# ScalarE's order inside a step of stick-breaking attention: exp and ln ahead of the upper part, the copy of the scores two steps ahead and behind it

## The chip, the cores and the metric

The kernel runs on one core of one Trainium2 chip. The metric is the device time of one execution in microseconds (us); lower is better. The engines are named as the profile names them: PE is TensorE (matmuls; PEld its weight loads), ACT is ScalarE, DVE is VectorE, POOL is GpSimd, SP is SyncE, which issues nearly all DMAs.

## The reference, cut to what matters

One decoder layer over 1024 positions and 1024 channels: RMSNorm, one wide input projection, three mixers (gated gMLP, gated DeltaNet, stick-breaking attention), a gated sum of their outputs, an output projection and a feed-forward part. The change touches only the attention:

```python
z = einsum('bthd,bshd->bhts', q, k) * dh ** -0.5            # 8 heads of 64
log_keep = where(causal, log_sigmoid(-z), 0)                # = -softplus(z)
later = cumsum(log_keep, axis=3, reverse=True) - log_keep
w = where(causal, exp(log_sigmoid(z) + later), 0)
o = einsum('bhts,bshd->bthd', w, v)
```

Here t is the query position, s the key position, and the sum runs over the keys between them.

## The kernel before, in words

Every matrix product in the kernel is done with three fp32r matmuls: each operand is split into an upper and a lower part, and high*high, high*low and low*high are added up. One core does everything, in phases. The second phase is the attention. It is a loop of four turns, each over two heads (u = 0, 1). A turn walks 12 blocks, `BLOCKS`: for queries 0 to 511 (T = 0) the key blocks j = 3, 2, 1, 0 of 128 keys, then for queries 512 to 1023 (T = 1) the key blocks 7 down to 0. A block has one step for each head, so a turn has 24 steps, `STEPS`. Step 2x and step 2x+1 belong to block x. A step's tiles are [128 keys, up to 512 queries]; on the diagonal only the queries that can see the keys are taken, so the widths by block are 128, 256, 384, 512, and again 128, 256, 384, 512, 512, 512, 512, 512.

The work of one step y goes around the engines like this (names as in the code, lines as in the profile):

- PE `scores` (L989 mask, L992): both steps of a block at once, into one of three PSUM banks `s_bank[y % 3]` each.
- ACT `copy_z` (L709): scores times 0.125 into `a_z[y % 4]`. It waits for the scores (`z_ready`), and from step 4 on for `argument(y - 4)`, which is the last reader of that buffer (`arg_ready`).
- DVE `minus_abs` (L1250): -|z| into `a_e[y % 3]`.
- ACT `exp_z` (L714) and `ln_z` (L719): ln(1 + exp(-|z|)), in place.
- DVE `softplus` (L1257): max(z, 0) plus that, into `a_sp`.
- ACT `upper_sp` (L726) and DVE `lower_sp` (L1263): the two fp32r parts of it.
- PE `sums_from` (L1002, L1003): the running sum over keys with a triangular matrix, and later `sums_rest` (L1010, L1011) for what the triangle left out.
- DVE `argument` (L1272): z minus the running sum, into `a_A`.
- ACT `exp_arg` (L732): its exp, the weights.
- PE `weighted_values` (L1021): once per block, two blocks later.

The orders in which the engines take these are written out by hand, and each engine keeps to its own. In loop turn y (28 of them, `NST + LAG`):

- DVE does `lower_sp(y-1)`, `argument(y-2)`, `minus_abs(y+1)`, `softplus(y)`.
- PE does `sums_rest(y-3)`, `sums_from(y-1)`, two or three steps (6 to 9 matmuls of 512 columns) of the input projection that runs beside the attention (`pe_beside`, L306 to L308), and in every even y also `weighted_values(y/2-2)` and then `scores(y/2+1)`.
- ACT does the order that the change edits, and now and then its share of the projection beside (`act_beside`): it takes half a block of results out of PSUM (`stage`, L332; behind y = 3, 6, 10, 13, 17, 20, 24, 27), and behind y = 6, 13, 20 and 27 also splits the next weights (`w_hi`, L294), which DVE's `w_lo` (L298) waits for.

Of the kernel before, what the change touches and what calls it, by code (L numbers as in the profile page):

```python
# [54 lines left out]
def hybrid_decoder_layer(nc, xT, w_stream, w_bd, w_spT, cols_in, consts_in, outT):  # L55
# [17 lines left out]
    with top:  # L73
# [343 lines left out]
        def act_beside(act, b):  # L417
            for step in b.steps():
                blk, r = divmod(step, 16)
                n, s = b.n0 + blk // 2, blk % 2  # L420
                if r == 7:
                    take_projection(act, n, s, 0, b.funcs[blk // 2])
                if r == 15:
                    take_projection(act, n, s, 1, b.funcs[blk // 2])
                    if b.funcs[blk // 2] == ACT.Gelu and s == 1:
                        exp_ln_tables()
                    split_hi(act, n + 1, s)
# [65 lines left out]
        NST = len(STEPS)  # L493
# [4 lines left out]
        def cols_of(y):  # L498
            return slice(first_col(STEPS[y][0], STEPS[y][2]), HALF)
# [159 lines left out]
        def _(act):  # L659
# [36 lines left out]
            with act.Fori(0, 4) as i:  # L696
                b = Beside(PAIR_AT + 2 * i, AT_SLOTS, (ACT.Identity,) * 2)
                act_beside(act, b)

                for hf in range(2):  # L700
                    act.wait_ge(at_vt, 2 * i + hf + 1)
                    nc.scalar.activation(a_v[:, 4 * hf:4 * hf + 4, :], z_bank[hf][:].rearrange("p (n c) -> p n c", c=P),
                                         ACT.Copy).then_inc(at_v, 1)

                def copy_z(y):
                    act.wait_ge(z_ready, 1 + NST * i + y + 1)
                    if y >= 4:
                        act.wait_ge(arg_ready, NST * i + y - 3)
                    nc.scalar.activation(a_z[y % 4][:, cols_of(y)], s_bank[y % 3][:, cols_of(y)], ACT.Copy, scale=0.125).then_inc(z_read, 1)  # L709

                def exp_z(y):
                    e = a_e[y % 3][:, cols_of(y)]
                    act.wait_ge(na_ready, NST * i + y + 1)
                    nc.scalar.activation(e, e, ACT.Exp).then_inc(e_ready, 1)  # L714

                def ln_z(y):
                    e = a_e[y % 3][:, cols_of(y)]
                    act.wait_ge(e_ready, NST * i + y + 1)
                    nc.scalar.activation(e, e, ACT.Ln, bias=1.0).then_inc(l_ready, 1)  # L719

                def upper_sp(y):
                    act.wait_ge(sp_ready, NST * i + y + 1)
                    if y >= 4:
                        act.wait_ge(cum_ready, NST * i + y - 3)
                        act.wait_ge(rest_done, N_REST * i + RESTS[y - 3])
                    nc.scalar.activation(a_sp_hi[y % 4][:, cols_of(y)], a_sp[y % 3][:, cols_of(y)], ACT.Copy).then_inc(sp_hi_ready, 1)  # L726

                def exp_arg(y):
                    T, u, j = STEPS[y]
                    act.wait_ge(arg_ready, NST * i + y + 1)  # L730
                    a = a_A[u][(y // 2) % 2][:, cols_of(y)]
                    nc.scalar.activation(a, a, ACT.Exp).then_inc(a_ready, 1)  # L732

                def out_av(T):
                    act.wait_ge(av_done, 2 + NBK * i + 4 * (2 * T + 1))
                    act.wait_ge(y_stored[T], 1 + 16 * i)
                    nc.scalar.activation(a_y[T][:], o_bank[:], ACT.Copy).then_inc(av_read, 1)
                    act.wait_ge(av_read, 1 + 2 * i + T + 1)
                    act.dma_start(yT[8 + i, :, HALF * T:HALF * T + HALF], a_y[T][:]).then_inc(y_stored[T], 16)

                copy_z(0)
                for y in range(NST + LAG):
                    if 1 <= y < NST + 1:
                        upper_sp(y - 1)
                    if y < NST:
                        exp_z(y)
                    if y + 1 < NST:
                        copy_z(y + 1)
                    if y < NST:
                        ln_z(y)  # L750
                    if 2 <= y < NST + 2:
                        exp_arg(y - 2)
                    act_beside(act, b)
                    if y == 11:
                        out_av(0)
                out_av(1)
# [875 lines left out]
```

## Time and profile before

| | |
|---|---|
| median of 3 runs | 2322.13 us (2322.05 to 2327.91) |
| profiled execution | 2324.92 us |
| its span, first to last instruction | 2323.1 us |
| mean granted TensorE clock | 0.955 of full speed |
| PE busy / DVE busy / ACT busy | 2112.4 / 906.6 / 814.1 us |
| attention, from the first copy of scores to the last `stage` | about 203.4 to 621 us, four turns of about 107 us |

Busy times are of the whole span; a matmul counts as busy until its modelled end, so a busy PE isn't one at its peak. The attention is 18% of the span; all else in the kernel is the same in both versions.

### The profile page before, as it was taken

Reading aid. Unit: us, or ns where it says so; the run is one execution under the profiler, and the core shown is the slowest. Engines: PE = TensorE matmul, PEld = TensorE weight load, DVE = VectorE, ACT = ScalarE, POOL = GpSimd, SP = SyncE. Lnnn points to the kernel's source line nnn. Section 1 sums busy time; section 2 is a strip of 40 time slices with the busy share of each in tenths; the row PEclk is TensorE's granted clock in tenths of the full one; section 3 lists DMA queues with packets and bytes.
Section 4 is the critical chain, followed back from the end, with each engine's and each line's share of the span. In section 5 each row is a group of like instructions: output and inputs, shape, how many; then the busy total and the mean of one; then the engine's idle time right before and its main releaser. Section 6 shows DMA issues by size and latency. Waiting matters only on the chain.

```text
span 2323.1 us, 26938 instructions
## 1 busy us (share of the span) xinstructions
PE 2112.4 (91%) x9786; PEld 1639.2 (71%) x9786; DVE 906.6 (39%) x1229; ACT 814.1 (35%) x1297; POOL 126.6 (5%) x79
## 2 busy tenths in 40 slices
PE   6998888888999999999979899977999999999994
PEld 3885555555678787877747688845888888888883
DVE  4113535354462534436223556245322322322335
ACT  4224646565633534334223433233301302302311
POOL 2000000000012030302100000022000000000002
PEclk7998999898999999999989999987999999999997
DMA  3222111212121212112042443311111111111113
GB/s 119 101 81 82 42 68 41 72 44 72 67 103 37 99 36 92 61 54 72 18 190 90 182 136 120 134 74 44 45 54 45 45 54 45 45 54 45 45 45 145
DMA packets 51530, 174.16 MB, mean 75 GB/s; under 512 B 5536, under 2 KB 5536, under 8 KB 51488
## 3 DMA queue, kind: packets, MB, share of 16 engines
q1 hardware_dynamic: 50336, 171.52, 20.7%
q10 hardware_dynamic: 1152, 2.10, 0.2%
q8 instruction: 25, 0.41, 0.1%
q14 instruction: 17, 0.14, 0.0%
HBM read 127.45 MB, written 46.14 MB: 75 GB/s over the span
## 4 chain that ended last, share of the span: by engine, by line
PE 67%; DVE 8%; ACT 5%; DMA 4%; issue 4%; SPq 1%; POOL 1%; ACTq 0%; DVEq 0%; POOLq 0%
PE gemm L306 16%; PE gemm L308 16%; PE gemm L307 16%; DMA w_raw<-w_stream 2%; PE dn L1091 2%; PE dn L1089 2%; PE gemm L1170 2%; PE gemm L1171 1%; PE gemm L1172 1%; PE attn_out L1021 1%; ACT w_hi L294 1%; DVE d_cv L1306 1%; PE z L992 1%; DMA a_k<-projections 1%; DVE a_sp_lo L1263 1%
## 5 line engine op out<-in xcount | busy, mean ns | idle before, releaser
L306 PE MATMUL gemm<-act_hi,w_hi 128*128 128x512 f32 x1600 | 667.1, 417 | 40.4 <-DVE act_lo L469 16.2
L308 PE MATMUL gemm<-act_hi,w_lo 128*128 128x512 f32 x1600 | 636.5, 398 | 0.0
L307 PE MATMUL gemm<-act_lo,w_hi 128*128 128x512 f32 x1600 | 636.2, 398 | 0.0
L306 PEld LDWEIGHTS gemm<-act_hi,w_hi 128*128 128x128 f32 x1600 | 307.5, 192 | 125.1 <-issue 36.7
L308 PEld LDWEIGHTS gemm<-act_hi,w_lo 128*128 128x128 f32 x1600 | 307.5, 192 | 67.5
L298 DVE TENSOR_TENSOR w_lo<-w_raw,w_hi 128x1024 fp32r<-128x1024 f32 x144 | 177.5, 1233 | 452.5 <-ACT w_hi L294 447.7
L307 PEld LDWEIGHTS gemm<-act_lo,w_hi 128*128 128x128 f32 x1600 | 308.8, 193 | 61.6 <-issue 6.5
L294 ACT ACTIVATE w_hi<-w_raw 128x1024 fp32r<-128x1024 f32 x144 | 151.4, 1052 | 334.6 <-PE gemm L308 281.5
L332 ACT ACTIVATE stage<-gemm,cols 128x512 f32<-128x512 f32 x120 | 82.2, 686 | 338.1 <-PE gemm L308 332.6
L306 PE MATMUL gemm<-f_hi,w_hi 128*128 128x512 f32 x512 | 199.2, 389 | 0.0
L307 PE MATMUL gemm<-f_lo,w_hi 128*128 128x512 f32 x512 | 199.2, 389 | 0.0
L308 PE MATMUL gemm<-f_hi,w_lo 128*128 128x512 f32 x512 | 199.2, 389 | 0.0
L1541 POOL TENSOR_TENSOR d_bB<-d_at,consts 128x512 f32<-128x512 f32 x48 | 64.4, 1356 | 993.3 <-DVE d_at L1352 905.8
L306 PEld LDWEIGHTS gemm<-f_hi,w_hi 128*128 128x128 f32 x512 | 96.1, 188 | 20.0
L307 PEld LDWEIGHTS gemm<-f_lo,w_hi 128*128 128x128 f32 x512 | 96.1, 188 | 20.0
L308 PEld LDWEIGHTS gemm<-f_hi,w_lo 128*128 128x128 f32 x512 | 96.1, 188 | 19.9
L1479 DVE TENSOR_TENSOR f_t<-f_t 128x512 f32<-128x512 f32 x64 | 44.3, 692 | 162.7 <-ACT f_t L908 162.7
L908 ACT ACTIVATE f_t<-gemm 128x512 f32<-128x512 f32 x64 | 38.3, 599 | 189.0 <-PE gemm L308 189.0
L1493 DVE TENSOR_TENSOR mixed<-mixed,gemm 128x512 f32 (+1 forms) x48 | 33.0, 688 | 175.3 <-PE gemm L308 175.2
L1250 DVE SCALAR_TENSOR_TENSOR a_e<-a_z 128x512 f32<-128x512 f32 (+3 forms) x96 | 53.4, 556 | 89.2 <-ACT a_z L709 88.2
L1170 PE MATMUL gemm<-y_hi,w_hi 128*128 128x512 f32 x192 | 77.3, 403 | 9.7 <-DVE y_lo L370 7.6
L1263 DVE TENSOR_TENSOR a_sp_lo<-a_sp,a_sp_hi 128x512 fp32r<-128x512 f32 (+3 forms) x96 | 53.5, 558 | 66.3 <-ACT a_sp_hi L726 66.3
(225 smaller groups left out, 2506.3 us busy)
## 6 DMA issues: line engine op xcount, KB each, us to landing
w_raw<-w_stream SPq DMA_DIRECT2D x144, 512.0 KB, 3.5
projections<-stage SPq DMA_DIRECT2D x60, 512.0 KB, 2.9
gate<-projections SPq DMA_DIRECT2D x48, 256.0 KB, 2.8
d_in<-projections SPq DMA_DIRECT2D x12, 512.0 KB, 4.5
y_lo<-branch_outputs SPq DMA_DIRECT2D x6, 1024.0 KB, 12.0
x_sb<-xT SPq DMA_DIRECT2D x4, 1024.0 KB, 8.6
x_fin<-xT SPq DMA_DIRECT2D x4, 1024.0 KB, 8.0
residual<-mixed SPq DMA_DIRECT2D x8, 512.0 KB, 2.6
```

The lines of the kernel that those rows point to most:

```text
L294: nc.scalar.activation(w_hi[s][:], w_raw[s][:].rearrange("p (k c) -> p k c", k=KT), ACT.Copy).then_inc(hi_ready[s], 1)
L298: nc.vector.tensor_tensor(w_lo[s][:], w_raw[s][:].rearrange("p (k c) -> p k c", k=KT), w_hi[s][:].bitcast(f32), ALU.subtract).then_inc(lo_ ...
L306: nc.tensor.matmul(g_bank[hf][:], w_hi[s][:, k, :], a_hi[:, k, t], start=(k == 0), stop=False)
L307: nc.tensor.matmul(g_bank[hf][:], w_hi[s][:, k, :], a_lo[:, k, t], start=False, stop=False)
L308: last = nc.tensor.matmul(g_bank[hf][:], w_lo[s][:, k, :], a_hi[:, k, t], start=False, stop=(k == KT - 1))
L332: nc.scalar.activation(stage[s][:, HALF * hf:HALF * hf + HALF], g_bank[hf][:], func, bias=cols[:, ds(V_BIN + 2 * n + s, 1)]).then_inc(bank ...
L1089: last = nc.tensor.matmul(o, d_B[:, n, :], d_T[:, n, :], start=True, stop=True)
L1091: last = nc.tensor.matmul(o, d_X[:, n, :], d_TT[:, n, :], start=True, stop=True)
L1170: nc.tensor.matmul(g_bank[hf][:], w_hi[s][:, kk, :], y_upper(y)[:, t], start=(k == 0), stop=False)
L1250: nc.vector.scalar_tensor_tensor(a_e[y % 3][:, t], z[:, t], -1.0, z[:, t], ALU.mult, ALU.min).then_inc(na_ready, 1)
L1263: nc.vector.tensor_tensor(a_sp_lo[y % 4][:, t], a_sp[y % 3][:, t], a_sp_hi[y % 4][:, t].bitcast(f32), ALU.subtract).then_inc(sp_lo_ready, 1)
L1541: nc.gpsimd.tensor_tensor(d_B[:, c, :], d_at[:, c, :], consts[:, None, C_LEV + lev, :].broadcast_to([P, 4, P]), ALU.mult).then_inc(dn_b[g], 1)
```

## The change

The order of ACT in loop turn y of the attention is another one. Before: `upper_sp(y-1)`, `exp_z(y)`, `copy_z(y+1)`, `ln_z(y)`, `exp_arg(y-2)`. After: `exp_z(y)`, `ln_z(y)`, `upper_sp(y-1)`, `copy_z(y+2)`, `exp_arg(y-2)`. The copy of step 1 moves ahead of the loop, beside that of step 0. No instruction is added or removed, and neither the waits that an operation carries nor the orders of PE, DVE, POOL and SP are edited.

```diff
                 copy_z(0)
+                copy_z(1)
                 for y in range(NST + LAG):
+                    if y < NST:
+                        exp_z(y)
+                        ln_z(y)
                     if 1 <= y < NST + 1:
                         upper_sp(y - 1)
-                    if y < NST:
-                        exp_z(y)
-                    if y + 1 < NST:
-                        copy_z(y + 1)
-                    if y < NST:
-                        ln_z(y)
+                    if y + 2 < NST:
+                        copy_z(y + 2)
                     if 2 <= y < NST + 2:
                         exp_arg(y - 2)
                     act_beside(act, b)
```

## Rows read from the trace of the kernel before

**Rows 1.** The page: busy time of the engines over the span.
```profile
PE 2112.4 (91%) x9786; PEld 1639.2 (71%) x9786; DVE 906.6 (39%) x1229; ACT 814.1 (35%) x1297; POOL 126.6 (5%) x79
```

**Rows 2.** Waits of PE, whole span: us in total, times, longest.
```profile
PE dn L1002 <- DVE a_sp_lo L1263: 25.3, 24, 3.3
...
PE cumsum L1002 <- DVE a_sp_lo L1263: 11.4, 8, 1.9
```

**Rows 3.** Timeline of all engines, second turn: start, duration in us, idle before it.
```profile
366.59 0.60 ACT L709 ACTIVATE a_z<-z 128x512 f32<-128x512 f32 x1 [0.80 <-PE dn L992]
...
368.63 0.63 ACT L726 ACTIVATE a_sp_hi<-a_sp 128x512 fp32r<-128x512 f32 x1 [0.51 <-DVE a_sp L1257]
...
369.29 0.69 DVE L1263 TENSOR_TENSOR a_sp_lo<-a_sp,a_sp_hi 128x512 fp32r<-128x512 f32 x1 [0.78 <-ACT a_sp_hi L726]
...
369.90 0.68 DVE L1272 TENSOR_TENSOR a_A<-a_z,cumsum 128x512 f32<-128x512 f32 x1
...
370.04 0.51 PE L1002 MATMUL dn<-a_sp_hi,a_from 128*128 128x512 f32 x1
...
371.10 0.68 DVE L1257 SCALAR_TENSOR_TENSOR a_sp<-a_z,a_e 128x512 f32<-128x512 f32 x1
...
371.90 0.63 ACT L726 ACTIVATE a_sp_hi<-a_sp 128x512 fp32r<-128x512 f32 x1 [0.59 <-DVE a_sp L1257]
...
374.03 0.60 ACT L709 ACTIVATE a_z<-z 128x512 f32<-128x512 f32 x1 [0.99 <-PE z L992]
...
374.53 0.62 ACT L719 ACTIVATE a_e<-a_e 128x512 f32<-128x512 f32 x1
...
375.27 0.68 DVE L1257 SCALAR_TENSOR_TENSOR a_sp<-a_z,a_e 128x512 f32<-128x512 f32 x1
```

**Rows 4.** Groups of ACT in 314 to 403 us: busy, mean ns, idle before.
```profile
L726 ACT ACTIVATE a_sp_hi<-a_sp 128x512 fp32r<-128x512 f32 x12 | 7.5, 628 | 4.5 <-DVE a_sp L1257 4.4
...
L714 ACT ACTIVATE a_e<-a_e 128x512 f32<-128x512 f32 x12 | 7.4, 616 | 0.0
L732 ACT ACTIVATE a_A<-a_A 128x512 f32<-128x512 f32 x11 | 6.9, 626 | 2.8 <-DVE a_A L1272 2.8
L332 ACT ACTIVATE stage<-gemm,cols 128x512 f32<-128x512 f32 x7 | 4.8, 688 | 5.7 <-PE gemm L308 5.7
...
L294 ACT ACTIVATE w_hi<-w_raw 128x1024 fp32r<-128x1024 f32 x3 | 3.1, 1046 | 0.0
...
L714 ACT ACTIVATE a_e<-a_e 128x128 f32<-128x128 f32 x4 | 1.2, 298 | 0.4 <-DVE a_e L1250 0.4
```

**Rows 5.** Timeline of ACT alone, second turn, its first and last block.
```profile
318.02 0.38 ACT L709 ACTIVATE a_z<-dn 128x256 f32<-128x256 f32 x1 [1.37 <-PE z L992]
...
319.10 0.31 ACT L726 ACTIVATE a_sp_hi<-a_sp 128x128 fp32r<-128x128 f32 x1 [0.49 <-DVE a_sp L1257]
...
393.43 0.63 ACT L726 ACTIVATE a_sp_hi<-a_sp 128x512 fp32r<-128x512 f32 x1 [0.65 <-DVE a_sp L1257]
```

**Rows 6.** Stretches: length, busy (x count) of PE, PEld, DVE, ACT, POOL, granted clock, DMA share, GB/s.
```profile
229.00:232.00 3.00, 3.00 (x9) 2.31 (x8) 1.82 (x5) 2.19 (x7) 0.00 (x0) 0.55 0.02 8
256.00:259.00 3.00, 3.00 (x10) 0.80 (x8) 1.16 (x2) 1.06 (x2) 0.00 (x0) 0.50 0.02 10
359.00:362.00 3.00, 0.60 (x4) 0.35 (x2) 0.85 (x2) 2.50 (x5) 0.00 (x0) 1.00 0.21 85
403.00:411.00 8.00, 8.00 (x34) 4.74 (x32) 0.00 (x0) 1.39 (x3) 0.00 (x0) 1.00 0.00 0
```

**Rows 7.** The chain that ended last, first turn, block 7 to 8.
```profile
254.19 0.44 PE dn L1002
...
259.45 0.59 ACT a_z L709
```

**Rows 8.** The same chain, second turn, the same place.
```profile
362.91 0.44 PE dn L1002
...
366.61 0.59 ACT a_z L709
```

## The prediction, made before the changed kernel was run

> **What bounds the kernel now.** I read the page first. PE is busy 91% of the span and ACT 35% [rows 1]. So ACT's order can matter only where PE waits for ACT. The waits view says where. In the attention PE waits for the running sum's operand, the lower part, 25.3 + 11.4 = 36.7 us in 32 waits [rows 2]. The reader should see in it that PE already follows a ring of ACT and DVE in this stage.
>
> The timeline gives the ring [rows 3]. Take a loop turn with even y = 16, all tiles 512 wide. `upper_sp(15)` starts at 368.63, `lower_sp(15)` at 369.29, `sums_from(15)` at 370.04. Behind it on PE stand the projection's matmuls, `weighted_values` and the scores of the next block. The copy of those scores, `copy_z(18)`, starts at 374.03, having waited for exactly them. Call the time from `upper_sp(y-1)` to `copy_z(y+2)` A; here A = 5.40 us. Then DVE, which keeps its order, does `minus_abs(18)` and `softplus(17)`, the latter from 375.27 to 375.95, and 0.12 later the next odd `upper_sp` could start (371.10 + 0.68 to 371.90 is that 0.12). So the way back, B, is 376.07 - 374.03 = 2.04 us, and the ring is A + B = 7.44. The copies of this block and the one before it start at 366.59 and 374.03, also 7.44 apart. The ring explains the time in full.
>
> **The change part by part.** Nothing is added or removed, so no duration enters on its own: the price is what stands behind what. The rule of the new order is that in an even turn `copy_z(y+2)` stands directly behind `upper_sp(y-1)`. Its scores come from PE's end of the same turn y, which needs that very `upper_sp(y-1)`. PE's order isn't edited, so A stays, and ACT now idles through nearly all of it. Before, ACT did `exp_z(y)`, `copy_z(y+1)`, `ln_z(y)`, `exp_arg(y-2)`, `upper_sp(y)` and `exp_z(y+1)` in that time and waited only 0.99 [rows 3]. All this now starts behind the copy, and `upper_sp(y)` with it, which DVE and PE wait for.
>
> The new way back B, at full width, from the start of `copy_z(y+2)`. Queued ACT instructions start 0.50 (behind a copy, 374.03 to 374.53) to 0.52 apart, 0.10 less than their 616 to 628 ns [rows 3, 4]. An instruction that needs the result before it starts 0.03 after its end (`upper_sp` to `lower_sp`: 0.66).
> - copy 0.50, `exp_arg(y-2)` 0.52, `exp_z(y+1)` 0.65 (ln needs it), `ln_z(y+1)` 0.52: `upper_sp(y)` starts at 2.19.
> - `lower_sp(y)` starts 0.66 later, at 2.85. DVE's `argument(y-1)` stands behind it, 0.61 later, at 3.46, and ends at 4.14 (0.68).
> - `copy_z(y+3)` overwrites the tile that `argument(y-1)` reads, so it waits for that: 0.11 later, 4.25. (Before, the copy ran one step ahead only, and this wait was long met.)
> - copy 0.50, `exp_arg(y-1)` 0.52, `exp_z(y+2)` 0.65, `ln_z(y+2)` 0.52: `upper_sp(y+1)` starts at 6.43. `minus_abs(y+2)` ended at 4.74, before its exp; `softplus(y+1)` is done too.
>
> So B goes from 2.04 to 6.43, and the ring from 7.44 to 11.83: 4.39 us more for each full block.
>
> Narrower blocks: an ACT instruction takes 298 ns at 128 columns against 616 at 512 [rows 4], the four widths lying on a line. In the above, by width 128/256/384/512, the terms of the copied block are 0.96/1.36/1.80/2.17, those of the block being argued 0.81/1.14/1.50/1.83, those of the block between 1.09/1.52/1.98/2.43. For blocks x = 1 to 10 this makes B = 4.13, 5.29, 4.89, 4.28, 4.13, 5.29, 6.10, 6.43, 6.43, 6.43, together 53.4. A, read off at the same ten places of the second turn as from 368.63 to 374.03 [rows 3], is 3.6, 4.5, 4.4, 5.3, 4.7, 4.5, 5.6, 5.4, 5.6, 5.6, together 49.1.
>
> ACT's share of the projection now lies wholly on the ring: six `stage` at 0.59 and three `w_hi` at 0.95 inside it (688 and 1046 ns less 0.10 [rows 4]), 6.4 us. In the odd turns y = 3, 13, 17 `stage` also waits about 0.4 for PE's late projection, 1.2. The output copy behind y = 11 costs 1.2, as it did. With 0.3 for the clock still low at the start, the ten rings take 53.4 + 49.1 + 6.4 + 1.2 + 1.2 + 0.3 = 111.6 us from `upper_sp(1)` to `upper_sp(21)`. Before it is 393.43 - 319.10 = 74.3 [rows 5]. That is 37.3 us more.
>
> Start: `copy_z(2)` stays at 318.02 (its scores aren't moved) [rows 5]. Now `exp_z(1)`, `ln_z(1)`, `upper_sp(0)`, `lower_sp(0)`, `minus_abs(2)`, `exp_z(2)`, `ln_z(2)` stand between it and `upper_sp(1)`, some 2.7 us at these widths, so that starts at 320.75 instead of 319.10: 1.65 more. `copy_z(1)` ahead of the loop costs nothing: ACT idled there.
>
> End: nothing. From `upper_sp(21)` on no copies are left, and PE has its two turns of matmuls and four of projection to do without a gap (8.00 busy of 8.00 in the last stretch [rows 6]); ACT's last `exp_arg` comes at 10.8 after `upper_sp(21)` by the steps above, PE asks for it at 13.9. DMAs: ACT's output store moves with its copy, weight loads and stores on SP are a turn ahead; all have more time, not less. The next heads' loads start at the end of the turn, as before, so the 10 us between turns stay.
>
> One turn: 37.3 + 1.65 = 39.0; four turns 156 us.
>
> **The clock.** PE's idle stretches grow. After the scores PE now waits for `lower_sp(y)`: 2.85 + 0.75 behind the copy less 0.46 of `sums_rest`, 3.1 us at full width, at least 2 in each narrower ring, and up to 4.6 where `w_hi` falls in, all against a longest wait of 3.3 before [rows 2]. The trace before shows both outcomes of such a wait. Behind those at 226 and 250 us the granted clock was 0.55 and 0.50, so the lower level of 1.2 GHz; behind the 3.3 us at 359 it stayed at 1.00 [rows 6]. I count four falls behind the eight waits of 1.9 us and more in the four turns (in each, one of 1.9 and one of 3.3 [rows 2]). The price is to be had from one place in two turns: from `sums_from` to the copy 259.45 - 254.19 = 5.26 with a fall, 366.61 - 362.91 = 3.70 without [rows 7, 8], so 1.6 us. Now there are ten such waits in a turn, 40 in all. With half of them followed by a fall, and half of the falls spent behind `sums_from(y)`, where PE has some 1.7 us to spare before `upper_sp(y+1)`, that is 10 x 1.6 = 16, less the four falls already in the time, 6: 10 us. Bounds: -6 (no fall any more) and 40 x 1.6 = 64.
>
> The Trainium skill ("TensorE: Matmul & The Clock Gate", on the oscillation of the gate in real kernels) goes further: it says that idle gaps between bursts of matmuls bring PE back to the half rate again and again, every burst starting cold. This case's rows agree only in part, since one of the two 3.3 us waits left the clock at 1.00. By the page the sum would be at the upper bound or the second rival below, not at 10.
>
> **Sum.** 2324.9 (profiled) + 156 + 10 = 2491 us. The median of the runs lies 2.8 lower, so I say 2490.
>
> **The rivals.**
> - *The clock never comes back.* The whole of A runs at 1.2 GHz in every ring. At full width A has 3.96 us of PE in it, some 2.5 of them matmul streaming that doubles; over the ten rings and four turns about 100 us. For it: half the waits before were followed by a fall. Against: after each fall the next three us were back at 1.00, and at the low clock PE idles less. Time 2325 + 156 + 100 = 2580.
> - *The second copy doesn't hold.* If `copy_z(y+3)` and what follows it is not held up by `argument(y-1)` (its wait is met in time because DVE is ahead of my steps), B is 1.5 shorter at full width, about 1.2 on average: 40 x 1.2 = 48 less, 2440. Against: `argument(y-1)` is queued behind `lower_sp(y)` on DVE, and that needs `upper_sp(y)`.
> - *Faster: the DVE detour vanishes.* Before, `softplus` stood behind `minus_abs` and so behind the late copy (B). With ln two steps from the copy, `upper_sp` no longer needs the new scores. If the scores were there when the copy's turn comes, PE would lose all its waits for the lower part, 36.7 us [rows 2]: 2288. It decides at one point: the scores must come within about 0.5 us after `upper_sp(y-1)`, and the 5.40 measured has PE's whole turn in it, which depends on this `upper_sp`. I see no way to that.
> - *Nothing changes*: the waits only swap places. The ring would have to be set by PE; but PE waited in it 32 times.
>
> **Chances and range.** The forecast as summed, 2460 to 2540: 0.62. Clock low throughout or nearly so, above 2540: 0.17. Second copy not held, or other steps shorter, 2400 to 2460: 0.15. Slower, but by less than that: 0.02. Faster 0.02, no change 0.02. A measurement of this kernel can tell 0.3%, 7 us, from no change. So slower 0.96, same 0.02, faster 0.02. The range for 8 in 10 takes the neighbours partly in: 2430 to 2560.
>
> **What the changed profile would show.** In even turns ACT idles 4 to 5 us for the scores (L992), directly behind `upper_sp` (L726), not about 1; the full-width copies of consecutive blocks start 11.8 apart without projection work; PE's waits at L1002 for `a_sp_lo` go from 36.7 us to somewhere between 110 and 190, with 3 us at a full block; each turn of the loop takes 39 us more and the span before 203 us and after the attention stays as it was. The second copy waits for `a_A` of DVE (L1272). The clock falls inside the four turns some 20 times, not four. If ACT does not wait right behind `upper_sp` in the even turns, the mechanism is wrong; if it does and the pitch isn't near 11.8, a term of B is.

## The result, and the profile after

| | before | changed |
|---|---|---|
| median of the runs | 2322.09 us (2321.42 to 2327.91, 4 runs) | 2515.58 us (2512.83 to 2519.29, 4 runs) |
| span of the profiled execution | 2323.1 us | 2511.0 us |
| mean granted TensorE clock | 0.955 | 0.925 |

The changed kernel is slower: ratio 1.0828, 95% interval 1.0806 to 1.0851, so 193 us more. The forecast was 2490 (range 2430 to 2560), 166 us more.

First the page of the changed kernel: the busy times of DVE, ACT and POOL are those of before [rows 1] within 1%. PE's reads 76 us more and its weight loads' 49 us more.

```profile
PE 2188.1 (87%) x9786; PEld 1688.1 (67%) x9786; DVE 902.9 (36%) x1229; ACT 820.8 (33%) x1297; POOL 126.6 (5%) x79
```

The instructions are as many as before, so single matmuls took longer, and that goes with the lower granted clock. The stretches (columns as in [rows 6]) show where: ahead of the attention and behind it PE is as busy as it was, for as long. First the changed kernel, then the one before.

```profile
0.00:199.00 199.00, 172.10 (x682) 131.86 (x683) 41.51 (x36) 59.94 (x77) 12.95 (x10) 0.91 0.28 101
811.00:2511.00 1700.00, 1576.25 (x7542) 1273.64 (x7541) 653.77 (x794) 500.88 (x681) 113.65 (x69) 0.97 0.22 77
199.00:811.00 612.00, 439.73 (x1567) 282.56 (x1566) 207.66 (x399) 259.96 (x540) 0.00 (x0) 0.81 0.11 38
```

```profile
0.00:200.00 200.00, 172.79 (x684) 131.74 (x685) 41.50 (x36) 60.18 (x78) 12.95 (x10) 0.91 0.28 102
621.00:2323.00 1702.00, 1578.54 (x7545) 1276.06 (x7543) 653.55 (x795) 501.17 (x681) 113.70 (x69) 0.97 0.22 77
200.00:621.00 421.00, 361.08 (x1561) 231.44 (x1560) 211.56 (x399) 252.77 (x539) 0.00 (x0) 0.94 0.15 55
```

The attention went from 421 to 612 us, and its granted clock from 0.94 to 0.81. Those 191 us are the whole loss. The waits of the changed kernel answer to [rows 2]: us in total, times, longest.

```profile
ACT a_z L709 <- PE z L992: 140.3, 32, 6.8
...
PE cumsum L1002 <- DVE a_sp_lo L1263: 122.3, 44, 4.5
...
ACT a_z L709 <- PE dn L992: 89.1, 16, 7.2
...
ACT a_z L709 <- DVE a_A L1272: 45.5, 40, 1.4
...
PE dn L1002 <- DVE a_sp_lo L1263: 28.0, 17, 3.8
```

PE's waits for the lower part went from 36.7 to 150.3 us, and ACT stands 229 us in front of copies waiting for scores (61 before). The third kind of wait on `a_z` is new: 40 times, once a ring, a copy waits for `argument`.

The timeline of one full-width ring in the changed kernel answers to [rows 3].

```profile
459.87 0.61 ACT L726 ACTIVATE a_sp_hi<-a_sp 128x512 fp32r<-128x512 f32 x1
...
466.94 0.60 ACT L709 ACTIVATE a_z<-dn 128x512 f32<-128x512 f32 x1 [6.46 <-PE z L992]
...
467.44 0.62 ACT L732 ACTIVATE a_A<-a_A 128x512 f32<-128x512 f32 x1
467.95 0.62 ACT L714 ACTIVATE a_e<-a_e 128x512 f32<-128x512 f32 x1
468.61 0.63 ACT L719 ACTIVATE a_e<-a_e 128x512 f32<-128x512 f32 x1
469.14 0.61 ACT L726 ACTIVATE a_sp_hi<-a_sp 128x512 fp32r<-128x512 f32 x1
469.79 0.69 DVE L1263 TENSOR_TENSOR a_sp_lo<-a_sp,a_sp_hi 128x512 fp32r<-128x512 f32 x1 [6.78 <-ACT a_sp_hi L726]
470.39 0.68 DVE L1272 TENSOR_TENSOR a_A<-a_z,dn 128x512 f32<-128x512 f32 x1
470.53 0.50 PE L1002 MATMUL cumsum<-a_sp_hi,a_from 128*128 128x512 f32 x1 [2.96 <-DVE a_sp_lo L1263]
...
471.17 0.60 ACT L709 ACTIVATE a_z<-z 128x512 f32<-128x512 f32 x1 [1.42 <-DVE a_A L1272]
...
473.37 0.61 ACT L726 ACTIVATE a_sp_hi<-a_sp 128x512 fp32r<-128x512 f32 x1
```

Read it downwards from the copy at 466.94. It comes directly behind an upper part (459.87) and a wait of 6.46 us. From there the second upper part starts at 2.20, its lower part at 2.85, `argument` at 3.45, the second copy at 4.23 behind a wait of 1.42, and the next upper part at 6.43. The prediction had 2.19, 2.85, 3.46, 4.25 and 6.43. So B is as worked out. But A is 7.07 us here, not 5.4 to 5.6: that is the clock, as the experiment e4 shows below.

### The profile page after: what moved, and what is told of

Its sections match the earlier page's. It is cut to its first block, busy times and chain, and to the rows that moved or that the text cites. A ratio compares the mean times of both kernels' runs of the same rounds, so it can differ in the third digit from the quotient of the medians.

```text
span 2511.0 us, 26938 instructions
## 1 busy us (share of the span) xinstructions
PE 2188.1 (87%) x9786; PEld 1688.1 (67%) x9786; DVE 902.9 (36%) x1229; ACT 820.8 (33%) x1297; POOL 126.6 (5%) x79
## 4 chain that ended last, share of the span: by engine, by line
PE 66%; ACT 8%; DVE 7%; issue 4%; DMA 4%; SPq 1%; POOL 1%; ACTq 0%; DVEq 0%; POOLq 0%
PE gemm L306 16%; PE gemm L307 15%; PE gemm L308 15%; DMA w_raw<-w_stream 2%; PE dn L1091 2%; PE attn_out L1021 2%; PE dn L1089 1%; PE gemm L1170 1%; PE gemm L1172 1%; PE gemm L1171 1%; PE z L992 1%; ACT a_sp_hi L726 1%; DVE a_sp_lo L1263 1%; ACT w_hi L294 1%; ACT a_e L714 1%
## 5 line engine op out<-in xcount | busy, mean ns | idle before, releaser
L306 PE MATMUL gemm<-act_hi,w_hi 128*128 128x512 f32 x1600 | 687.0, 429 | 40.3 <-DVE act_lo L469 16.2
L308 PE MATMUL gemm<-act_hi,w_lo 128*128 128x512 f32 x1600 | 655.4, 410 | 0.0
L307 PE MATMUL gemm<-act_lo,w_hi 128*128 128x512 f32 x1600 | 655.3, 410 | 0.0
L306 PEld LDWEIGHTS gemm<-act_hi,w_hi 128*128 128x128 f32 x1600 | 319.7, 200 | 128.6 <-issue 37.0
L308 PEld LDWEIGHTS gemm<-act_hi,w_lo 128*128 128x128 f32 x1600 | 319.3, 200 | 72.0
L307 PEld LDWEIGHTS gemm<-act_lo,w_hi 128*128 128x128 f32 x1600 | 320.8, 200 | 64.8 <-issue 6.5
L1002 PE MATMUL cumsum<-a_sp_hi,a_from 128*128 128x512 f32 (+3 forms) x48 | 25.7, 536 | 122.3 <-DVE a_sp_lo L1263 122.3
L1002 PEld LDWEIGHTS cumsum<-a_sp_hi,a_from 128*128 128x128 f32 x48 | 10.5, 220 | 138.2 <-DVE a_sp_lo L1263 138.2
```

What stands on the lines that cost most here:

```text
L306: nc.tensor.matmul(g_bank[hf][:], w_hi[s][:, k, :], a_hi[:, k, t], start=(k == 0), stop=False)
L307: nc.tensor.matmul(g_bank[hf][:], w_hi[s][:, k, :], a_lo[:, k, t], start=False, stop=False)
L308: last = nc.tensor.matmul(g_bank[hf][:], w_lo[s][:, k, :], a_hi[:, k, t], start=False, stop=(k == KT - 1))
```

## The experiments

For each kernel A and B were read from the timeline at the ten rings (x = 1 to 10) of all four turns and summed. A is the time from an odd step's upper part to the late copy, B the way back to the next odd step's upper part. "Low clock" is the time at the lower level, added up from stretches of 1 us over the attention; "falls" are separate low stretches inside the turns, not counting the one that every turn begins with.

| kernel | median us | ratio to before | A, 40 rings | B, 40 rings | low clock, us | falls |
|---|---|---|---|---|---|---|
| before | 2322 | 1 | 211.5 | 92.1 | 52 | 4 |
| changed | 2515.6 | 1.0828 | 230.8 | 256.9 | 235 | 44 |
| e1, order alone | 2360.6 | 1.0164 | 222.9 | 118.5 | 75 | 9 |
| e2, depth alone | 2482.5 | 1.0688 | 228.4 | 228.4 | 202 | 34 |
| e3, late copy half a ring on | 2366.2 | 1.0193 | 219.8 | 124.2 | 71 | 9 |
| e4, PE kept busy | 2488.7 | 1.0725 | 209.9 | 249.4 | 84 | 11 |
| e5, five a_z tiles | 2498.8 | 1.0764 | 224.9 | 249.1 | 204 | 39 |
| e10, exp_arg first | 2479.6 | 1.0701 | 219.7 | 234.2 | 163 | 23 |

**Order or depth.** The change does two things: it puts exp and ln ahead of the upper part, and it copies two steps ahead. e1 and e2 do one each.

```diff
 # e1: order alone
+                    exp_z(y); ln_z(y)
                     upper_sp(y - 1)
-                    exp_z(y); copy_z(y + 1); ln_z(y)
+                    copy_z(y + 1)
 # e2: depth alone
+                copy_z(1)
...
-                        copy_z(y + 1)
+                        copy_z(y + 2)
```

> The order alone: exp, ln, upper part, then the copy only ONE step on (y+1), exp_arg. Theory (the copy of the scores in an even turn stands directly behind the upper part that those scores depend on, so ACT's work can't overlap PE's): here the late copy stands in the odd turn again, with exp, ln and the next upper part ahead of it, so A stays overlapped. Only minus_abs, exp and ln now lie between copy and next upper part: B = 0.63 + 0.79 + 0.65 + 0.52 = 2.6 instead of 2.04, 0.55 x 40 rings = 22 us, about 2345. Rival (exp and ln ahead of the upper part are what costs): near the changed kernel, 2480 to 2515.

> The depth alone: the old order (upper part, exp, copy, ln, exp_arg), but the copy is that of step y+2. Theory: in even turns the late copy again stands behind the upper part that its scores depend on, and ln(y), exp_arg, upper(y) wait behind it. By the steps of the prediction B = 5.98 at full width against 6.43 in the changed kernel, 0.45 x 40 = 18 us less than the changed kernel's 2516: about 2498. Rival (the order is what costs): near 2322 to 2345.

e1 took 2360.6 us (ratio 1.0164, interval 1.0146 to 1.0182), e2 2482.5 (1.0688, 1.0667 to 1.0709). The depth is what costs: alone it makes 162 of the 193 us, the order alone 40 (both against 2320.9 us, the kernel before measured beside them). Both numbers missed by some 15, e1 above and e2 below what was expected. In e1 B at full width is 2.56 (2.6 expected), but in the rings of the odd turns y = 3, 13 and 17, which have a `stage` in them, it grew by 1.0 to 1.2: B is 26 more in all (22 expected), A 11 more. In e2 B at full width is 5.94 (5.98 expected); what it is below the expectation comes mostly from the ring of y = 13, 6.5 to 8.1 where the changed kernel has 9.1 to 9.3, and that of y = 17. Two long waits on ACT stand in the timeline of a full-width ring of e2:

```profile
441.06 0.60 ACT L709 ACTIVATE a_z<-z 128x512 f32<-128x512 f32 x1 [4.26 <-PE z L993]
...
445.06 0.60 ACT L709 ACTIVATE a_z<-z 128x512 f32<-128x512 f32 x1 [0.90 <-DVE a_A L1273]
```

The wait for the scores is 4.26, against 4.98 in a ring of the changed kernel at full clock, since exp(y) now runs in it. Where the late copy stands decides more than the order of the rest.

**Half a ring.** e3 keeps the changed kernel's order and its total depth, and takes only the copy that waits for new scores out of the even turn.

```diff
-                    if y + 2 < NST:
-                        copy_z(y + 2)
+                    if y % 2 and y + 1 < NST:
+                        copy_z(y + 1)
+                        copy_z(y + 2)
```

> The changed kernel with one instruction moved by half a ring: the even turn's copy(y+2) is taken at the same place of the following odd turn, ahead of that turn's own copy(y+2); the even turn has none. Theory: exp_arg, exp, ln and the next upper part run during A again; B = 2.7 (two copies, exp_arg, exp, ln), 0.65 x 40 = 26 us over before: about 2348. Rival (the second copy's wait for argument, or exp and ln first, is the main cost): 2450 or more.

e3 took 2366.2 us (1.0193, 1.0176 to 1.021). One instruction moved by a turn of the loop gives back 149 of 193 us. In its timeline the second copy comes with no wait of its own, since the second upper part, its lower part and `argument` were done during A:

```profile
382.83 0.61 ACT L726 ACTIVATE a_sp_hi<-a_sp 128x512 fp32r<-128x512 f32 x1
385.63 0.60 ACT L709 ACTIVATE a_z<-z 128x512 f32<-128x512 f32 x1 [2.19 <-PE dn L993]
386.13 0.59 ACT L709 ACTIVATE a_z<-dn 128x512 f32<-128x512 f32 x1
```

This is the place of the loss, shown by taking it away. The time is 18 us above what was expected, which stays open in part: of the 45 us over the kernel before, B makes 32 (26 expected) and A 8 (none expected).

**The clock.** e4 adds matmuls whose results nobody reads, ahead of `sums_from`.

```diff
+                    if 3 <= y < NST - 1:
+                        keep_awake(y if y % 2 else y - 1, 9 if y % 2 else 5)
                     if 1 <= y < NST + 1:
                         sums_from(y - 1)
...
+                def keep_awake(y, count):
+                    pe.wait_ge(z_read, NST * i + y + 1)
+                    for _ in range(count):
+                        nc.tensor.matmul(s_bank[y % 3][:], a_from[:], act_hi[:, 0, 0:HALF], start=True, stop=True, ...)
```

> The changed kernel plus matmuls that nobody reads (9 in each odd turn, 5 in each even turn, 512 columns, ahead of sums_from), placed where PE idles, into the score bank whose copies are done. Theory: some 35 us of the 193 is the granted clock, which falls in the idle stretches and makes A longer (A sums to 54 to 60 us in a turn against 49 forecast); with PE busy the falls go and the time is 2475 to 2485. Rival 1 (the falls are spent where PE has time to spare): 2510 to 2520. Rival 2 (the added matmuls delay sums_from more than the clock gives back): above 2520.

e4 took 2488.7 us (1.0725, 1.0707 to 1.0743). More work made it 27 us faster, which ends 4 us above the expected range. The falls went from 44 to 11, A from 230.8 to 209.9, B from 256.9 to 249.4. The timeline is of the same ring as the one shown above: from upper part to late copy 5.59 us instead of 7.07, and the wait for the scores 4.98 instead of 6.46. The 9 added matmuls stand in what was an idle stretch of 2.96.

```profile
450.17 0.61 ACT L726 ACTIVATE a_sp_hi<-a_sp 128x512 fp32r<-128x512 f32 x1
...
455.76 0.60 ACT L709 ACTIVATE a_z<-dn 128x512 f32<-128x512 f32 x1 [4.98 <-PE z L992]
...
456.23 2.22 PE L1030 MATMUL z<-act_hi,a_from 128*128 128x512 f32 x9
...
459.36 0.50 PE L1002 MATMUL cumsum<-a_sp_hi,a_from 128*128 128x512 f32 x1 [0.91 <-DVE a_sp_lo L1272]
```

**The terms of B.** e5 takes the second copy's wait away, with a fifth `a_z` tile (all `y % 4` of it become `y % 5`); e10 moves `exp_arg(y-2)` ahead of the copy.

```diff
 # e5
-                    if y >= 4:
-                        act.wait_ge(arg_ready, NST * i + y - 3)
+                    if y >= 5:
+                        act.wait_ge(arg_ready, NST * i + y - 4)
 # e10
+                    if 2 <= y < NST + 2:
+                        exp_arg(y - 2)
                     if y + 2 < NST:
                         copy_z(y + 2)
-                    if 2 <= y < NST + 2:
-                        exp_arg(y - 2)
```

> The changed kernel with five a_z tiles instead of four, so that copy(y+3) no longer waits for argument(y-1). By the steps of B that wait costs little: copy(y+3) starts at 2.71 instead of 4.25, but exp_arg(y-1) behind it waits for the same argument, until 4.25, where it stood at 4.75. B 5.94 instead of 6.43, 0.49 x 40 = 20 us less than the changed kernel: about 2496. Rival (the prediction's second rival as it was priced, 1.2 to 1.5 a ring): 2456 to 2468.

> The changed kernel with exp_arg(y-2) ahead of copy(y+2). A check of the bookkeeping of B: in the even turn exp_arg runs while ACT would wait for the scores anyway, one slot of 0.52 less behind the copy at full width (0.2 to 0.5 by width). In the odd turn nothing changes, since both wait for argument(y-1). B 5.9 instead of 6.43, some 0.4 x 40 = 16 us less than the changed kernel: about 2500. Rival (B isn't a plain sum of what stands behind the copy): no change, 2516.

e5 took 2498.8 us (1.0764, 1.0748 to 1.078), 17 less than the changed kernel. The timeline shows why so little: the copy is early, and `exp_arg` behind it takes up the wait.

```profile
311.85 0.58 ACT L709 ACTIVATE a_z<-z 128x512 f32<-128x512 f32 x1
313.30 0.63 ACT L732 ACTIVATE a_A<-a_A 128x512 f32<-128x512 f32 x1 [0.87 <-DVE a_A L1272]
```

B there is 5.97 at full width (5.94 expected).

e10 took 2479.6 us (1.0701, 1.0659 to 1.0744), 36 less where 16 were expected. B at full width is 5.85, as worked out. Over 40 rings B gives 23, of it 7 in the rings of y = 13 (7.5 instead of 9.1 to 9.3), and A gives 11. There are 21 falls fewer. Why moving `exp_arg` spares falls was not tested.

**A faster kernel.** Four versions start from the kernel before. All swap `softplus` and `minus_abs` on DVE, so that the next upper part doesn't wait for the late copy by way of DVE.

```diff
 # DVE, all four
+                    if y < NST:
+                        softplus(y)
                     if y + 1 < NST:
                         minus_abs(y + 1)
-                    if y < NST:
-                        softplus(y)
 # ACT in e6: upper_sp(y-1), exp_z(y), ln_z(y), exp_arg(y-2), copy_z(y+1)
 # e7: copy_z(y+1) ahead of exp_arg(y-2)
 # e8: as e6, and act_beside of turn y-1 behind exp_z(y)
 # e9: as e8, and ahead of the wait for vT_loaded 22 matmuls that nobody reads
```

> A try at a faster kernel, from the ring of the one before: DVE takes softplus(y) ahead of minus_abs(y+1), and ACT takes upper(y-1), exp(y), ln(y), exp_arg(y-2), copy(y+1). The way from the late copy through minus_abs and softplus to the next upper part (B = 2.04) shrinks to one ACT slot, 0.5; then PE sets the pitch, some 6.75 by its own starts against 7.44. 0.7 x 40 = 28 us less at most, the waits behind stage and w_hi stay: about 2297. Rival (PE or the clock already sets the pitch): 2315 to 2325.

> As e6, but with the copy ahead of exp_arg, so B is 1.02 instead of 0.5. If the ring through ACT still sets the pitch this is some 0.3 to 0.5 a ring slower than e6, 2310; if PE does, the two are equal within 5 us.

> As e6, but ACT's share of the projection (stage, w_hi) of turn y is done in turn y+1 behind the upper part and exp, where PE no longer waits for it. The two long waits of a turn, 1.9 and 3.3 us, go, 5.2 x 4 = 21 us, and with them the four falls of the clock, 6: about 2272. Rival (these waits hide behind PE's own work or come back as a wait of DVE's w_lo): as e6.

> The kernel of e8 with 22 matmuls that nobody reads in the wait for the next heads' values between two turns (some 5 us of 5.5). The clock should then be at its upper level for the transposes, the first scores and the first projection steps, which ran at the lower one: some 6 to 7 us of PE work at half rate in e8's trace, 2 to 3 us less a turn, 8 to 10 in all: about 2300. Rival (a DMA or ACT sets this stretch): as e8, 2309.

| kernel | median us | ratio to before | interval |
|---|---|---|---|
| e6 | 2313.4 | 0.9962 | 0.9948 to 0.9976 |
| e7 | 2314.5 | 0.9964 | 0.9950 to 0.9978 |
| e8 | 2309.1 | 0.9942 | 0.9930 to 0.9955 |
| e9 | 2308.7 | 0.9940 | 0.9920 to 0.9959 |

All four beat the kernel before, by 0.4 to 0.6%, but e6, e8 and e9 by far less than expected. e7 equals e6, so the 0.5 us that its B is longer doesn't reach the time; the expectation read that as PE setting the pitch, which the two times alone don't show. In e6 B at full width is 0.49, as wanted, and still PE's waits for the lower part are 32.3 us, against 36.7 [rows 2]:

```profile
PE dn L1001 <- DVE a_sp_lo L1262: 20.9, 16, 3.3
...
PE cumsum L1001 <- DVE a_sp_lo L1262: 11.4, 8, 1.9
```

The time from `upper_sp(1)` to `upper_sp(21)`, four turns together, is 304.0 us in e6's profiled execution against 303.7 before: what the shorter B gave came back as a longer A. Most of the 5.5 us that this execution's span is shorter lies ahead of it, from copy 0 to `upper_sp(1)`: 16.9 us in four turns against 20.6. The longest waits (3.3 and 1.9) are as long as before. In e8, which moves ACT's `stage` and `w_hi` behind the upper part, PE still waits 29.1 us, and the 3.3 is still there. Its trace says where it comes from:

```profile
352.98 0.52 ACT L726 ACTIVATE a_sp_hi<-a_sp 128x384 fp32r<-128x384 f32 x1
...
356.43 1.23 DVE L298 TENSOR_TENSOR w_lo<-w_raw,w_hi 128x1024 fp32r<-128x1024 f32 x1 [2.61 <-ACT w_hi L294]
357.57 0.55 DVE L1265 TENSOR_TENSOR a_sp_lo<-a_sp,a_sp_hi 128x384 fp32r<-128x384 f32 x1
...
358.17 0.44 PE L1004 MATMUL dn<-a_sp_hi,a_from 128*128 128x384 f32 x1 [3.32 <-DVE a_sp_lo L1265]
```

The upper part is there at 353.5, but on DVE `w_lo` stands ahead of `lower_sp` and waits 2.61 us for `w_hi`. So the wait came back through `w_lo`, the rival that e8's expectation names. It does so twice in every turn (2.50 and 3.32 us), which makes 23 of the 29 us. That `w_lo` must move with `w_hi` is a reading of this trace; no run here moves it.

e9 equals e8: the added matmuls kept the clock up for the transposes only, and in its chain of 296 to 316 us the keys' transfer `a_k` takes 32.8%, so a DMA sets that stretch, as the rival had it.

## Why the prediction was right, and what was off

- *What bounds the kernel.* Right. The ring of A and B is what moved, and nothing else: A +19, B +165, the start of the turns (copy 0 to `upper_sp(1)`, 20.6 to 26.4) +6, together 190 us, against 188 us more span.
- *The mechanism.* Right, and shown from both sides: the depth alone makes the loss (e2), and the late copy alone, taken half a ring on, undoes three quarters of it (e3).
- *B.* Right within 4%: with its share of the projection 62.2 us a turn were forecast, 64.2 measured. Most of the difference is the ring with y = 13, 9.1 to 9.3 instead of 7.2: `stage` waits there for PE's projection, 2.17 us in the second turn. With PE kept busy (e4) it waits 0.86, and this ring's B is 7.8.
- *The second rival* (second copy not held, 48 us less) was priced wrongly. e5 makes its condition true and gives 17. What I had overlooked is that `exp_arg` behind the copy waits for the same `argument`, so the term to take off was 0.49, not 1.2.
- *The clock.* This term was mis-sized. +10 was forecast. e4 gives 27 us back with 11 falls left, and in the sum of A and B over 40 rings it is 28 below the changed kernel. By difference the term is 35: the 40 rings took 184.0 us more than before, and the sum without the clock had 4 x 37.3 = 149.2. (A's +19 hides part of it: before, `stage` and `w_hi` of y = 6 stood in A, and now they stand in B.) I let half of 40 waits be followed by a fall, 20; there were 44 falls. My assumption that half of their price is spent where PE has time held roughly: 33 falls fewer gave 28 us, 0.85 each, about half of 1.6.
- The page of the Trainium skill that stood against the small clock term ("TensorE: Matmul & The Clock Gate", on oscillation in real kernels) was nearer than my reading of one wait that left the clock alone: the trace agrees that bursts between gaps start cold again and again, with 44 falls in 40 rings. Its strong form, the first rival with A wholly at 1.2 GHz (2580; the prediction calls it the second where it speaks of the page), did not come: in each turn at least five of the ten A stayed within 0.5 of what the forecast had.
- *Base.* The forecast took all four turns as the second; the other three took 1.6 to 3.3 us longer, 6.4 together, which is what was taken off under the clock for the four falls already there (6).
- *The signs.* PE's waits for the lower part (150.3, 110 to 190 said), 3 us of them at a full block (2.96), and the copies' waits directly behind the upper part came as said, though up to 7.2 us long and not 4 to 5. A turn took 47 us more, not 39, and 44 falls came, not 20. The last sign was badly put: the ring shown is 13.50 long and not 11.83, and that isn't a term of B (6.43) but the 1.67 that A is longer.

One ring shows what the clock term is. Stretches of the changed kernel, columns as in [rows 6]:

```profile
453.00:456.00 3.00, 0.40 (x2) 0.00 (x0) 0.38 (x1) 2.55 (x5) 0.00 (x0) 1.00 0.00 0
458.00:464.00 6.00, 4.68 (x12) 3.15 (x11) 2.60 (x5) 2.45 (x5) 0.00 (x0) 0.50 0.00 0
464.00:467.00 3.00, 3.00 (x12) 0.98 (x11) 0.00 (x0) 0.06 (x1) 0.00 (x0) 0.92 0.00 0
```

PE idled most of the first, and six microseconds at the lower level followed, from 458; they reach beyond `upper_sp` at 459.87 into A, which made it 7.07. In the ring before, at full clock, the upper part at 447.17 and the copy at 452.77 are 5.60 apart:

```profile
447.17 0.61 ACT L726 ACTIVATE a_sp_hi<-a_sp 128x512 fp32r<-128x512 f32 x1
452.77 0.60 ACT L709 ACTIVATE a_z<-z 128x512 f32<-128x512 f32 x1 [4.98 <-PE z L992]
```

## What to carry to other kernels

An engine with one queue pays for a wait with all that stands behind it. Before moving an instruction ahead in such an order, ask which other engine's turn produces its operand and what that turn in turn waits for: if that is the instruction just ahead of it, the two engines take turns instead of overlapping. Here a copy one step deeper gained nothing, because the scores that it copies come no earlier (e2, 162 us more).

A ring written as a sum of starts, from rows, can be forecast closely: here B at full width was 6.43 us in both. Then look at what grows idle, since PE's idle time cost once more through the clock (27 us, e4). And when a wait is taken away, look at the next instruction in the queue for the same operand (e5), and at the other engines that do a part of the same job (`w_lo` in e8).

## What the runs showed of the hardware that was not expected

- Useless matmuls made a kernel faster: 14 of them per ring, PE's idle stretches filled, falls from 44 to 11 and 27 us less (e4).
- The length of a wait alone did not decide whether the clock fell. Before, the waits of 3.3 us at `sums_from` kept the clock in three turns of four, and the waits of 1.9 us lost it in three of four.
- Filling a wait of 5.5 us between two turns with 22 matmuls gave nothing (e9): the clock stayed up for the transposes (8 in 1.09 us against 1.97) and was down to 0.81 in the six microseconds behind them, in which PE waited 2.2 us for a transfer.
